# A hybrid decoder step on one core: token norm in three groups, and the last expert's transposes moved

## The reference, cut to what matters

```python
def decoder_layer(x, conv_hist, attn_fn, norm1_g, w_in, ...):
    h = rms_norm(x, norm1_g)                       # x * rsqrt(mean(x*x) + eps) * g
    z = h @ w_in
    cb, cc, ch, q, k, v, ga, gb = jnp.split(z, IN_OFFSETS, axis=-1)
    ...
    x = x + mix @ w_o
    x = x + hier_moe(rms_norm(x, norm2_g), ...)    # top 2 of 32 experts for each token
    return x, ...
def run_block(args):                               # one expert on its tokens
    xb, e = args
    return (jax.nn.silu(xb @ w_gate[e]) * (xb @ w_up[e])) @ w_down[e]
...
y_prompt = rms_norm(hp, norm_f_g)
```

## Time and profile before

| | us |
|---|---|
| median of three runs | 1690.22 (1689.3 to 1690.39) |
| the profiled execution | 1687.95 |
| its span, first to last instruction | 1686.4 |
| PE busy in the span | 1614.6 |

### The profile page before, as it was taken

The page is one execution under the profiler, slowest core; times in us unless marked ns, Lnnn a source line. Parts: engine busy times, 40 slices in busy tenths (PEclk is TensorE's granted clock), DMA queues, the critical chain, the costliest instruction groups (busy, mean ns, idle before and its releaser), DMA issues. The chain is left out here.

```text
span 1686.4 us, 26201 instructions
## 1 busy us (share of the span) xinstructions
PE 1614.6 (96%) x9427; PEld 1470.6 (87%) x9427; DVE 1103.3 (65%) x1967; ACT 847.6 (50%) x1234; POOL 252.7 (15%) x245
## 2 busy tenths in 40 slices
PE   5999999999999999999999999799999999999991
PEld 4999999999999999999999887678888888877871
DVE  5332588888887232124224666898998998988883
ACT  6011366666665221122113211678878878777773
POOL 1111011110110000000000111332232232222310
PEclk9999999999999999999999999899999999999996
DMA  5252111111112111141113712999999999999956
GB/s 150 72 138 78 55 51 51 50 50 37 50 50 88 30 44 45 50 146 44 49 50 141 276 76 93 365 384 373 375 376 378 377 371 382 370 369 365 364 204 224
DMA packets 131856, 305.30 MB, mean 181 GB/s; under 512 B 30403, under 2 KB 92079, under 8 KB 106935
## 3 DMA queue, kind: packets, MB, share of 16 engines
q1 hardware_dynamic: 115415, 267.76, 43.4%
q0 software_dynamic: 16384, 36.76, 7.5%
HBM read 282.81 MB, written 40.41 MB: 192 GB/s over the span
## 5 line engine op out<-in xcount | busy, mean ns | idle before, releaser
L1956 DVE TENSOR_TENSOR e_lo<-e_raw,e_hi 128x2048 fp32r<-128x2048 f32 x192 | 434.1, 2287 | 58.7 <-ACT e_hi L1373 57.1
L1373 ACT ACTIVATE e_hi<-e_raw 128x2048 fp32r<-128x2048 f32 x192 | 366.1, 1921 | 63.6 <-PE bank L1059 28.3
L1162 ACT ACTIVATE w_hi<-w_raw 128x1024 fp32r<-128x1024 f32 x68 | 71.6, 1054 | 323.0 <-DMA w_raw<-in_w_in_dram 180.3
L1482 DVE TENSOR_TENSOR w_lo<-w_raw,w_hi 128x1024 fp32r<-128x1024 f32 x68 | 83.2, 1224 | 200.7 <-ACT w_hi L1162 200.7
L1057 PE MATMUL bank<-e_hi,xT_hi 128*128 128x512 f32 x512 | 206.1, 402 | 4.4 <-DVE xT_lo L1967 4.3
L723 PE MATMUL bank<-h_hi,w_hi 128*128 128x344 f32 x624 | 202.7, 325 | 1.1 <-DVE h_lo L1501 1.1
L1059 PE MATMUL bank<-e_hi,xT_lo 128*128 128x512 f32 x512 | 201.5, 394 | 0.0
L1058 PE MATMUL bank<-e_lo,xT_hi 128*128 128x512 f32 x512 | 201.5, 394 | 0.0
L724 PE MATMUL bank<-h_lo,w_hi 128*128 128x344 f32 x624 | 199.8, 320 | 0.0
L725 PE MATMUL bank<-h_hi,w_lo 128*128 128x344 f32 x624 | 199.7, 320 | 0.0
L869 PE MATMUL bank<-h_hi,w_hi 128*128 128x344 f32 x576 | 190.2, 330 | 0.0
(11 more groups left out here) (341 smaller groups left out, 3184.3 us busy)
## 6 DMA issues: line engine op xcount, KB each, us to landing
e_raw<-in_w_e_gate_dram SPq DMA_DIRECT2D x64, 1024.0 KB, 17.7
e_raw<-in_w_e_up_dram SPq DMA_DIRECT2D x64, 1024.0 KB, 18.4
e_raw<-in_w_e_down_dram SPq DMA_DIRECT2D x64, 1024.0 KB, 18.9
w_raw<-in_w_in_dram SPq DMA_DIRECT2D x104, 256.0 KB, 3.2
a_spill<-y_sb POOLq DMA_DIRECT2D x8, 516.0 KB, 4.0
a_raw<-a_spill SPq DMA_DIRECT2D x2, 2064.0 KB, 12.9
x_tok<-in_x_prompt_dram SPq DMA_DIRECT2D x4, 1024.0 KB, 10.8
w_raw<-in_w_attn_out_dram SPq DMA_DIRECT2D x32, 128.0 KB, 2.9
```

The lines of the kernel that those rows point to most:

```text
L1373: A.activation(e_hi[:, slot % 4, :], e_raw[slot][:, :], ACT.Copy).then_inc(e_hi_done, 1)
L1482: V.tensor_tensor(w_lo[:, slot, :, :], w_raw[slot][:, :, :], w_hi[:, slot, :, :].bitcast(F32), ALU.subtract).then_inc(lo_ready, 1)
L1956: V.tensor_tensor(e_lo[slot][:, :], e_raw[slot][:, :], e_hi[:, slot % 4, :].bitcast(F32), ALU.subtract).then_inc(e_lo_done, 1)
```

## The change

At the front the tokens form three groups of three tiles. SP loads tile 0, tiles 1 and 2, then unit 0's weights, then tiles 3 to 5, 6 and 7, and 8. ACT and DVE share the squares (DVE takes tiles 1 and 4, `square_in`); ACT calls a root on a dummy first. Each group's transposes (`turn_in`) use five banks in turn; the first five feature blocks are turned ahead, the last three behind the products of unit 0's chunk for that group of tokens, which now runs right behind its group. Chunk 0 needs group 0, chunk 1 groups 0 and 1, chunk 2 groups 1 and 2. `turn_new` goes. PE multiplies the identity with itself 10 times in front of group 0, 28 times in front of group 1's transposes and 20 times behind the first five of these. The bias heads begin behind unit 1's first chunk: 12 amid the chunks and four at the end. ACT takes the roots, the weight splits and the high parts in the order written out below.

At the end, `turn_act(31)` stands between the two halves of expert 30's down product, expert 31's activations get buffers of their own (`last_hi`, `last_lo`), and ACT makes the high part (`a_split(31)`) ahead of `store_rows(30)`.

```diff
@@ constants and buffers
-        junk = at("junk", R5, [D])
+        junk, junk2 = at("junk", R5, [D]), at("junk2", R5 + 12288, [D])
+        X_TILES = ((0,), (1, 2), (3, 4, 5), (6, 7), (8,))
+        x_of = [g for g, tiles in enumerate(X_TILES) for n in tiles]
...
+        last_hi, last_lo = at("last_hi", RING, [4, P], F32R), at("last_lo", RING + 2048, [4, P], F32R)
...
-        rest_done, REST_FROM = h_hi_done, 16
+        rest_done, REST_FROM = h_hi_done, 24
+        squared, SQUARED_FROM = dve_step, 1
@@ block.sync
-            for g in range(4):
-                sp.dma_start(x_tok[:, 2 * g:2 * g + 2, :],
-                             x_prompt[0, 256 * g:256 * g + 256, :].rearrange("(t p) d -> p t d", p=P)).then_inc(x_loaded[g], 16)
-            sp.dma_start(x_tok[0:B8, 8, :], x_sample[:, 0, :]).then_inc(x_loaded[4], 16)
...
-            for j in range(4):
+            for g, tiles in enumerate(X_TILES):
+                if g == 2:
+                    q_unit(0, 0, 0, None)
+                a, b = tiles[0], tiles[-1] + 1
+                if g < 4:
+                    sp.dma_start(x_tok[:, a:b, :], x_prompt[0, P * a:P * b, :].rearrange("(t p) d -> p t d", p=P)).then_inc(x_loaded[g], 16)
+                else:
+                    sp.dma_start(x_tok[0:B8, 8, :], x_sample[:, 0, :]).then_inc(x_loaded[g], 16)
+            for j in range(1, 4):
                 q_unit(0, j, j % 3, 3 if j == 3 else None)
@@ block.tensor
-            for g in range(2):
-                pe.wait_ge(x_scaled, 4 * g + 4)
+            for _ in range(10):
+                pe.matmul(bank[0][:, 0:P], ident, ident, start=True, stop=True)
+
+            def keep_warm(times):
+                for _ in range(times):
+                    pe.matmul(DN[2][:, 0:P], ident, ident, start=True, stop=True)
+
+            def turn_in(g, k):
+                q = KT * g + k
+                pe.wait_ge(x_scaled, 3 * g + 3)
+                if q >= 5:
+                    pe.wait_ge(h_lo_done, q - 4)
+                for i in range(3):
+                    n = 3 * g + i
+                    r = P if n < 8 else B8
+                    mm = pe.transpose(bank[3 + q % 5][:, P * i:P * i + r], x_tok[0:r, n, P * k:P * k + P], ident[0:r, 0:r])
+                mm.then_inc(xT_ready, 1)
+
+            for g in range(3):
+                cols = slice(CH * g, CH * g + CH)
+                if g == 1:
+                    keep_warm(28)
+                for k in range(5):
+                    turn_in(g, k)
+                if g == 1:
+                    keep_warm(20)
                 for k in range(KT):
-                    if g:
-                        pe.wait_ge(h_lo_done, k + 1)
-                    for i in range(4):
-                        mm = pe.transpose(bank[k][:, P * i:P * i + P], x_tok[:, 4 * g + i, P * k:P * k + P], ident)
-                    mm.then_inc(xT_ready, 1)
-
-            def turn_new():
-                pe.wait_ge(x_scaled, 9)
-                pe.wait_ge(h_lo_done, 12)
-                for k in range(KT):
-                    mm = pe.transpose(bank[3][:, B8 * k:B8 * k + B8], x_tok[0:B8, 8, P * k:P * k + P], ident[0:B8, 0:B8])
-                mm.then_inc(xT_ready, 1)
-
-
-            pe.wait_ge(h_lo_done, 9)
+                    pe.wait_ge(h_lo_done, KT * g + k + 1)
+                    if g == 0 and k == 0:
+                        pe.wait_ge(lo_ready, 1)
+                    pe.matmul(DN[g][:, 0:CH], w_hi[:, 0, k, :], h_hi[:, k, cols], start=k == 0, stop=False)
+                    pe.matmul(DN[g][:, 0:CH], w_hi[:, 0, k, :], h_lo[:, k, cols], start=False, stop=False)
+                    mm = pe.matmul(DN[g][:, 0:CH], w_lo[:, 0, k, :], h_hi[:, k, cols], start=False, stop=k == KT - 1)
+                    if k + 5 < KT:
+                        turn_in(g, k + 5)
+                mm.then_inc(chunk_done, 1)
 
...
             def units_a(t, first):
-                for i in range(5):
+                for i in range(1 if first else 0, 5):
                     u = t * 5 + i
                     pe.wait_ge(lo_ready, u + 1)
                     for c in range(3):
-                        if not (first and i == 0):
-                            pe.wait_ge(chunk_out, u * 3 + (c - 2))
-                        if first and i == 0 and c:
-                            pe.wait_ge(h_lo_done, 15 + c)
+                        pe.wait_ge(chunk_out, u * 3 + (c - 2))
                         unit_chunk((0, 1, 2, 0, 1)[i], h_hi, h_lo, c)
-                        if first and i == 0 and c == 0:
-                            turn_new()
-                        if first and (i or c):
-                            if i == 0 and c == 1:
+                        if first:
+                            if i == 1 and c == 0:
                                 pe.wait_ge(relb_split, 1)
-                            bias_head(3 * i + c - 1)
+                            bias_head(3 * i + c - 3)
 
             units_a(0, True)
-            bias_head(14)
-            bias_head(15)
+            for h in range(12, HEADS):
+                bias_head(h)
...
-            def chunk_d(s, slot, c):
+            def chunk_d(s, slot, c, a_hi=aT_hi, a_lo=aT_lo):
...
-                chunk_d(s, slot, 0)
-                chunk_d(s + 1, slot + 1, 1)
+                last = isinstance(e, int) and e == NE - 1
+                parts = (last_hi, last_lo) if last else (aT_hi, aT_lo)
+                chunk_d(s, slot, 0, *parts)
+                if isinstance(e, int) and e == NE - 2:
+                    turn_act(NE - 1)
+                chunk_d(s + 1, slot + 1, 1, *parts)
...
             step_e(31, 1, 184, 4, True, False)
-            turn_act(31)
             down_e(31, 190, 10)
@@ block.scalar
             act.wait_ge(relb_ones, 1)
-            for g in range(3):
-                for n in range(4 * g, min(4 * g + 4, NT)):
-                    rows = P if n < 8 else B8
-                    act.wait_ge(x_loaded[n // 2], 16)
-                    step.after(A.activation(junk[0:rows, :], x_tok[0:rows, n, :], ACT.Square, accum_out=ssq[0:rows, n:n + 1]))
-                rows, w = (P, 4) if g < 2 else (B8, 1)
-                A.activation(rms[0:rows, 4 * g:4 * g + w], ssq[0:rows, 4 * g:4 * g + w], ACT.Sqrt, bias=eps[0:rows, 0:1],
-                             scale=1.0 / D).then_inc(sqrt_done, 1)
+            A.activation(warm[:, :], eps[:, :], ACT.Sqrt)
+
+            def square_in(n):
+                rows = P if n < 8 else B8
+                act.wait_ge(x_loaded[x_of[n]], 16)
+                step.after(A.activation(junk[0:rows, :], x_tok[0:rows, n, :], ACT.Square, accum_out=ssq[0:rows, n:n + 1]))
+
+            def root_in(g):
+                if g < 2:
+                    act.wait_ge(squared, SQUARED_FROM + 2 * g + 1)
+                A.activation(rms[:, 3 * g:3 * g + 3], ssq[:, 3 * g:3 * g + 3], ACT.Sqrt, bias=eps[:, 0:1], scale=1.0 / D).then_inc(sqrt_done, 1)
+
+            def high_in(g):
+                w = 3 * P if g < 2 else 2 * P + B8
+                for k in range(KT):
+                    q = KT * g + k
+                    act.wait_ge(xT_ready, q + 1)
+                    A.activation(h_hi[:, k, 3 * P * g:3 * P * g + w], bank[3 + q % 5][:, 0:w], ACT.Copy, scale=g1[:, k:k + 1]).then_inc(h_hi_done, 1)
+
+            square_in(0)
+            square_in(2)
+            root_in(0)
+            split_hi(0, 1)
             act.wait_ge(start_copied, 1)
-            for g in range(2):
-                for k in range(KT):
-                    act.wait_ge(xT_ready, KT * g + k + 1)
-                    A.activation(h_hi[:, k, 512 * g:512 * g + 512], bank[k][:, :], ACT.Copy, scale=g1[:, k:k + 1]).then_inc(h_hi_done, 1)
-                if g == 0:
-                    split_hi(0, 1)
-
-
-            for slot, uses in ((1, 1), (2, 1), (0, 2), (1, 2), (0, 3), (1, 3), (2, 2), (0, 4), (1, 4)):
+            high_in(0)
+            for n in (3, 5):
+                square_in(n)
+            root_in(1)
+            for n in (6, 7, 8):
+                square_in(n)
+            root_in(2)
+            high_in(1)
+            split_hi(1, 1)
+            high_in(2)
+            for slot, uses in ((2, 1), (0, 2), (1, 2), (0, 3), (1, 3), (2, 2), (0, 4), (1, 4)):
                 split_hi(slot, uses)
...
             def a_split(e):
                 act.wait_ge(aT_psum, e + 1)
-                A.activation(aT_hi[:, :, :], bank[6][:, :].rearrange("p (k t) -> p k t", k=4), ACT.Copy).then_inc(aT_hi_done, 1)
+                dst = last_hi if isinstance(e, int) and e == NE - 1 else aT_hi
+                if dst is last_hi:
+                    act.wait_ge(e_used, 184)
+                A.activation(dst[:, :, :], bank[6][:, :].rearrange("p (k t) -> p k t", k=4), ACT.Copy).then_inc(aT_hi_done, 1)
...
             step_e(31, 1, 184, 4, 240)
+            a_split(31)
             store_rows(30, 190)
-            a_split(31)
             store_rows(31, 192)
@@ block.vector
             dve.wait_ge(start_psum, 1)
```

(57 more changed lines are left out.)

4 lines of the change are left out of this document (2 added, 2 removed).

## The result

| | before | changed |
|---|---|---|
| five runs each, median | 1689.43 | 1695.97 (1691.21 to 1697.52) |
| their ratio | | 1.0038, 95% interval 1.0028 to 1.0049 |
| a second set (run `y4_after_again` below) | 1688.66 | 1692.85, ratio 1.0022, 1.0012 to 1.0033 |
| the profiled execution, its span | 1687.95, 1686.4 | 1695.97, 1694.4 |

The change makes the kernel slower, by 0.2 to 0.4%. The first set lies above the forecast range (1687.0 to 1694.0), the second inside it. No change, with 0.80, was the wrong forecast.

A forecast was written before the change was run, and what follows sets the result against it. PE was taken to bound the kernel. The front's -0.2 us and the end's +0.15 were rounded to nothing: 1687.9 us for the profiled execution, median 1690.2, range 1687.0 to 1694.0.

The forecast's parts named there:

- No change: Whole kernel: time within 0.2% of the kernel before, chance 0.80; 0.53 for the case as worked out.
- What bounds the kernel: PE, busy 1614.6 of 1686.4 us; its gain or loss by unit 1's first product goes straight through.
- The overrun: Ahead of chunk 1: the 28 and 20 identity products outlast their waits, starting chunk 1 5.2 us later.
- the front's sum, -0.2: Up to the end of the bias heads: 44.3 + 0.7 - 45.2 = -0.2 us against the kernel before.
- The start: Front up to chunk 0: identity products from 9.0, group 0 scaled at 13.0, chunk 0 ended at 20.15 us.
- the upper bound that I gave: Front: landing of unit 0's weights at 13.3 us at the latest; 12.5 was taken.
- The short transposes: Group 2's first fifteen transposes, a third of 8 rows: 1.6 us; +1 if those cost full ones or worse.
- Chunk 2 and the constants: Before unit 1: last low part at 42.05, then DVE's constants 1.7 us and copy 0.52, so start at 44.3.
- The heads: Two more bias heads stand back to back at the end of the row, costing 0.7 us in all.
- The slow clock: Rival, front: clock rise missed at 13.1, chunk 0 at half rate, +2.05 to +4.75 us; chance 0.13.
- The end: Expert 31's last down product starts 0.8 us earlier, but ACT's last copy awaits expert 30's scatter: 0.15 us lost.
- the bounds of the front: Front: early weights -0.45, chunk 2 as last wait -0.7; weights at 13.3 +0.8, 8-row transposes +1 us.

The follow-up runs named there:

- `y4_after_again`: The changed kernel measured and profiled once more, nothing altered: 1692.85 us, ratio 1.0022 to the kernel before.
- experiment 4: The changed kernel with unit 0's weights issued behind all x tiles again, as in the kernel before: 1703.3 us, ratio 1.0091.
- experiment 6: Old end in the changed kernel, single execution: 1694.97 us; then the new end alone in the kernel before: 1688.52 us, ratio 1.0000.
- experiment 3: The changed kernel without the ten identity products in front, 28 and 20 kept: 1695.48 us, ratio 1.0034.
- experiment 1: The changed kernel without its 28 and 20 identity products, the ten in front kept: 1691.4 us, ratio 1.0008.
- experiment 8: Changed kernel with 14 and 11 products, constants ahead, heads spread, old end: 1687.51 us; also tile 2 scaled on ACT, eight products in front: 1687.87, then 1686.5.

## Why the prediction was wrong

**What bounds the kernel** was right: PE's shift of the front stays to the end, apart from the clock and from single waits of 0.9 us.

**The overrun** was right in kind and a little too large: "With no identity product PE could start chunk 1 there; it starts at 32.5, 5.2 us later." Measured, the 28 and 20 hold chunk 1 back by 4.7 us; they took 6.24 and 4.39 (6.2 and 4.45). They turn a front of -1.23 into one of +3.6 to +3.8.

**The step that failed is the front's sum, -0.2: three of its terms were too small, by 4.1 us together.**

- *The start, 1.9 us.* "PE starts its ten identity products at 9.0": 10.51, since POOL's rows, which I had let keep their time, landed 1.5 us later (PE's first transpose at 9.93; it was 8.43 before, by the copy at 8.76). Four profiles with the old front have this transpose at 8.24 to 8.86, twelve with the new one at 8.98 to 10.92, so the delay belongs to the change; how much of it is due to the weights' small pieces isn't shown (experiment 4: 9.11 with the weights behind). For tile 2 I had "another half is 1.3 us at 411 GB/s": tiles 1 and 2 landed at 10.3, where that gave 7.9, and at 9.2 even with the weights behind them. The rate was taken from 11 to 15 us; the earlier trace rows already show that the second MB took from 6.6 to 11.75. Either landing is enough to hold group 0: in the profile with the old end (experiment 6) the rows came at 9.16, and PE still waited for the scaling until 14.73. Unit 0's weights landed at 13.3, the upper bound that I gave. Chunk 0 ended 1.91 late, and 0.9 to 2.3 late over the nine profiles with this start.
- *The short transposes, 1.0 us.* "Group 2's first fifteen transposes, a third of them of 8 rows, 1.6": 2.56. A block of two full ones and one of 8 rows took 0.52 us, one of three full ones 0.33. The bound that I kept (+1) was the value.
- *Chunk 2 and the constants, 1.2 us.* The three blocks turned amid chunk 2 have such transposes too: products of one block to the next 1.05 instead of 0.80 us. The last low part so ended at 46.0, not 42.05, and the constants with the copies behind it set unit 1's start, as forecast; taking them ahead gave back 1.0.

**The heads** at the end: +0.7 forecast, +0.65 measured (3.19 to 3.84).

**The slow clock**, as a rival, did not come true where I put it: in the changed kernel PE's passes and transposes start 0.213 us apart to 15.58 and 0.110 from 15.77 on, so the clock rose 5.2 us after PE's first identity product, ahead of chunk 0. The 4.1 us that I carried over from the trace before didn't hold: over the seventeen profiles the spacing falls 2.9 to 6.2 us after the first of these products or transposes (3.9 in experiment 3, which has no identity products ahead of it). Half speed stood at 104.5 instead, in one of two profiles, and cost 1.5 us that no case of mine had.

**The end** was right: 0.15 us loss forecast, 0.33 measured, 0.23 with the new end alone. The last down product's gain (0.65, forecast 0.8) goes to the wait for the scatter.

**The chances.** I took the bounds of the front to offset each other, though each late landing and each dear transpose points the same way; of the loss of 4.2 to 6.5 us, 3.6 to 3.8 is the front, 0.3 the end, and up to 1.5 the clock behind the heads. In the first set some 0.9 us stay without an account.

## What to carry to other kernels

Work put into a wait to keep a clock up is itself on the path from the moment the wait ends; size it by the releaser's end in a trace and not by what the engine could hold. Before a transfer is moved ahead, look up what small transfer starts the stage and give its landing a range (here 8.98 to 10.92 us from one execution to the next), and take the rate of a transfer from the microseconds in which it will run: 411 GB/s held from 11 to 15 us, and ahead of that 1 MB took 5 us. And when two engines' waits meet at a buffer, shortening one only pays up to the other: here the scatter's 6 us.

## What the hardware showed unexpectedly

- TensorE's granted clock fell while it had no wait: in the changed kernel it was busy 9.40 of 9.40 us ahead of 104.4, with heads of 33 rows and transposes of 16 as its last work, and then ran 3.41 us at half speed. The Trainium skill (TensorE: Matmul & The Clock Gate, HAM oscillation) names idle stretches of TensorE as what lowers the clock. The falls at 26.7 in experiment 1 and at 20.2 in experiment 4, each with a wait of 3 us or more just ahead of it or around it, agree with that; this one does not.
- The old end has half speed at 1646 to 1657 us in three of seven profiles, at a cost of some 1.5 us (15.9 instead of 14.4 for the stretch of experiment 6); the new end in none of ten. PE's wait there is 2.13 us with the old and 1.40 with the new. If these counts hold, the old end costs 0.6 us on average, more than the new end's 0.3, and the version of experiment 8 might do better with the new one. I didn't test this further.
- A transpose of 8 rows amid full ones costs more than a full one: 0.52 us for a block with one against 0.33. Eight of them in a row took 0.66 us together in the kernel before (L752, at 35.56), so it is the mixture that is dear; why isn't shown.
